# A two-layer decoder trunk on one core: the forgetting-attention half reordered, its last head overlapped with the output projection, and the last strip and norm done by token halves

## The reference, cut to what matters

```python
h = concat(meta_tokens (16), x (512))                  # 528 tokens, D_MODEL 1024
h = gla_layer(h, ...)                                  # gated linear attention, 4 heads: not touched
k, v, f_logit = split(rmsnorm(h, kv_norm_g) @ w_kv)    # 16 heads of 128
cum = cumsum(log_sigmoid(f_logit + b_forget))          # per head, over tokens
q, r = split(rmsnorm(h, norm_g) @ w_in, 2)
s = q @ k^T * 128**-0.5 + cum[q] - cum[k]              # causal
o = softmax(s) @ v                                     # per head
h = h + (o * silu(r)) @ w_out                          # 2048 -> 1024
out = rmsnorm(h, final_norm_g)[:, 16:]
```

## Time and profile before

| | |
|---|---|
| time before, median of 3 (lowest to highest) | 1192.83 us (1192.6 to 1192.99) |
| profiled execution: its own time, and its span from first to last instruction | 1195.57 us, 1193.8 us |
| PE, matmuls busy | 1107.8 us, 93% of the span |
| DVE busy, ACT busy | 612.2 us (51%), 496.3 us (42%) |
| mean granted TensorE clock | 0.965 of full |
| largest part of the chain that ended last | PE L1138, 68% |

### The profile page before, as it was taken

How to read it: one execution, slowest core, us unless ns; L and a number is a source line. 1 busy time by engine, 2 the same in 40 slices (tenths; PEclk the granted TensorE clock), 3 DMA queues, 4 the chain that set the end, 5 groups by cost and what they waited for, 6 DMA issues and landing times.

```text
span 1193.8 us, 18411 instructions
## 1 busy us (share of the span) xinstructions
PE 1107.8 (93%) x7716; PEld 1011.7 (85%) x7716; DVE 612.2 (51%) x1032; ACT 496.3 (42%) x869; POOL 0.2 (0%) x4
## 2 busy tenths in 40 slices
PE   6897999799799999999799999999999999998995
PEld 5786998799799899998688888888888888886883
DVE  5664473556457437535445554455455555564233
ACT  5624523723452325424434444444444444454221
POOL 0000000000000000000000000000000000000000
PEclk9898999899999999999899999999999999998997
DMA  6111121112112111222111222112211212211211
GB/s 224 53 54 36 54 89 54 42 65 89 37 54 80 63 54 57 103 89 71 54 66 59 71 71 71 57 68 72 71 57 68 71 55 70 72 56 51 92 50 70
DMA packets 23762, 81.77 MB, mean 68 GB/s; under 512 B 2784, under 2 KB 3040, under 8 KB 23680
## 3 DMA queue, kind: packets, MB, share of 16 engines
q1 hardware_dynamic: 23680, 80.59, 19.4%
HBM read 78.49 MB, written 2.10 MB: 68 GB/s over the span
## 4 chain that ended last, share of the span: by engine, by line
PE 83%; DVE 9%; ACT 4%; issue 3%; DMA 0%; DVEq 0%; ACTq 0%; SPq 0%
PE psum L1138 68%; PE psum L1378 3%; PE psum L1364 2%; PE psum L1207 2%; DVE w_lo L684 2%; ACT w_hi L348 1%; DVE y L691 1%; PE psum L1347 1%; PE psum L1361 1%; PE psum L1349 1%; PE psum L1350 1%; PE psum L1348 1%; DVE y L845 1%; DVE gsr L691 1%; DVE y_lo L691 1%
## 5 line engine op out<-in xcount | busy, mean ns | idle before, releaser
L684 DVE TENSOR_TENSOR w_lo<-raw,w_hi 128x1024 fp32r<-128x1024 f32 x144 | 174.9, 1220 | 81.9 <-ACT w_hi L348 81.7
L1138 PE MATMUL psum<-xh,w_hi 128*128 128x264 f32 x768 | 165.1, 297 | 35.6 <-DVE y L845 27.9
L348 ACT ACTIVATE w_hi<-raw 128x1024 fp32r<-128x1024 f32 x144 | 149.9, 1048 | 100.0 <-PE psum L1138 100.0
L1138 PE MATMUL psum<-xl,w_hi 128*128 128x264 f32 x768 | 161.0, 292 | 0.0
L1138 PE MATMUL psum<-xh,w_lo 128*128 128x264 f32 x768 | 160.0, 291 | 0.0
L1138 PEld LDWEIGHTS psum<-xh,w_hi 128*128 128x128 f32 x768 | 124.3, 197 | 40.8 <-DVE w_lo L684 29.1
L1138 PEld LDWEIGHTS psum<-xl,w_hi 128*128 128x128 f32 x768 | 124.3, 196 | 0.0
L1138 PEld LDWEIGHTS psum<-xh,w_lo 128*128 128x128 f32 x768 | 124.2, 196 | 0.0
L1138 PE MATMUL psum<-zh,w_hi 128*128 128x264 f32 x512 | 106.2, 289 | 5.9 <-DVE y L691 3.2
L1138 PE MATMUL psum<-zl,w_hi 128*128 128x264 f32 x512 | 104.4, 286 | 0.0
L1138 PE MATMUL psum<-zh,w_lo 128*128 128x264 f32 x512 | 104.1, 285 | 0.0
(11 more groups left out here) (239 smaller groups left out, 1896.8 us busy)
## 6 DMA issues: line engine op xcount, KB each, us to landing
raw<-w_all SPq DMA_DIRECT2D x144, 512.0 KB, 3.2
hT<-xT SPq DMA_DIRECT2D x8, 264.0 KB, 5.4
outT<-hT SPq DMA_DIRECT2D x8, 256.0 KB, 2.3
cst<-consts SPq DMA_DIRECT2D x1, 528.0 KB, 6.9
y<-w_up_ SPq DMA_DIRECT2D x2, 64.0 KB, 8.1
low_raw<-w_low SPq DMA_DIRECT2D x1, 64.0 KB, 2.1
f_raw<-w_f SPq DMA_DIRECT2D x1, 64.0 KB, 8.2
vec<-vecs SPq DMA_DIRECT2D x1, 22.5 KB, 1.6
```

Of the source, the lines that this page charges most:

```text
L348: nc.scalar.activation(w_hi[:, n % HI_RING, :], raw[:, n % LO_RING, :], ACT.Copy).then_inc(hi_made, 1)
L684: nc.vector.tensor_tensor(w_lo[:, n % LO_RING, :], raw[:, n % LO_RING, :], w_hi[:, n % HI_RING, :].bitcast(F32), ALU.subtract).then_inc(lo ...
L1138: i = nc.tensor.matmul(o, w[a][:, k % KT, :], x[b][:, k, c0:c1], start=k == first and a == b == 0, stop=k == last and a == 1)
```

## The change

Five things are changed.

1. **Prologue.** `q0` moves from the end of the prologue to a place right behind `LOWF`; the chunk order follows. `LOWF` gets its own place in banks 6 and 7. On ACT the last `x2h` (a part of the input of q) is made ahead of the square root; on DVE the last `x2l` and four memsets stand ahead of the reciprocal of the norm; the gate's Abs and Exp stand ahead of `keys_hi(0)`; `queries_hi(0)` and `queries_lo(0)` stand ahead of the last steps of the gate.
2. **Attends in their own bank.** `a{h}` always goes to bank 7; the other jobs alternate without it (`PLACE`, `BEFORE`). Bank 7 also holds scores, so `fox_scores(h+1)` now waits for `y` of head h (`fy_made`).
3. **Transposes.** `transpose_probs` does the ten large ones first, then the four small ones, and signals once instead of five times.
4. **Last head.** `w0`'s k-tiles 0 to 7 run between `r15` and the transposes, its k-tiles 8 to 14 between transposes and attend; then come `w1`'s 0 to 14, and then k-tile 15 of both. `z_high` and `z_low` move: 0 to 3 ahead of `q15` and 4 to 7 at the end of head 14, 8 to 14 ahead of `probs_hi(15)` and `probs_lo(15)`, and 15 alone at the end.
5. **Tail.** `w7` is computed for tokens 0 to 255 and then for 256 to 511 in a second bank (96 matmuls of 256 columns instead of 48 of 512), and add, square, sum, root, reciprocal, multiplications and stores are done per half. There are still eight stores of 256 KB; each now takes two feature tiles of half the tokens, in runs of 1 KB instead of 2 KB.

The core of the diff (the matching moves on ACT are left out, they follow the description above):

```diff
@@ -91,11 +92,23 @@
 
 
 JOBS = (["LOW"] + [j for h in range(GLA_HEADS) for j in gla_jobs(h)] + [f"W{d}" for d in range(KT)]
-        + ["k0", "LOWF", "v0", "x0", "v1", "q0"] + [j for h in range(FOX_HEADS) for j in fox_step(h)] + [f"w{d}" for d in range(KT)])
+        + ["k0", "LOWF", "q0", "v0", "x0", "v1"] + [j for h in range(FOX_HEADS) for j in fox_step(h)] + [f"w{d}" for d in range(KT)])
 JOB = {j: n for n, j in enumerate(JOBS)}
+PLACE, BEFORE = {}, {}
+_slots = 0
+for _job in JOBS:
+    if _job[0] == "a":
+        PLACE[_job] = 7
+    elif _job == "LOWF":
+        PLACE[_job] = 6
+    else:
+        PLACE[_job] = 2 * (_slots % 2)
+        _slots += 1
+    _same = [j for j in PLACE if PLACE[j] == PLACE[_job]]
+    BEFORE[_job] = _same[-2] if len(_same) > 1 else None
 
 CHUNKS = ([c for h in range(GLA_HEADS) for c in gla_strips(h)] + [f"W{d}{half}" for d in range(KT) for half in "ab"]
-          + ["k0", "v0", "v1", "q0"] + [j for h in range(FOX_HEADS) for j in fox_step(h) if j[0] in "rkqv"]
+          + ["k0", "q0", "v0", "v1"] + [j for h in range(FOX_HEADS) for j in fox_step(h) if j[0] in "rkqv"]
           + [f"w{d}{half}" for d in range(KT) for half in "ab"])
 CHUNK = {c: n for n, c in enumerate(CHUNKS)}
...
+            for half in range(2):
+                c0 = half * HS
+                for d in range(0, KT, 2):
+                    sp.wait_ge(final_made, half * KT + d + 2)
+                    sp.dma_start(out[:, d:d + 2, c0:c0 + HS], hT[:, d:d + 2, META + c0:META + c0 + HS]).then_inc(stored, 16)
             sp.wait_ge(stored, 16 * KT)
...
-                                                   op0=ALU.mult, op1=ALU.subtract).then_inc(x2l_made, 1)
-            done(dve, f"W{KT - 1}")
+                dve.wait_ge(x2h_made, d + 1)
+                nc.vector.scalar_tensor_tensor(x2l[:, d, :], hT[:, d, META:T], vec[:, G_NORM1 + d:G_NORM1 + d + 1], x2h[:, d, :].bitcast(F32),
+                                               op0=ALU.mult, op1=ALU.subtract).then_inc(x2l_made, 1)
             H = FOX_HEADS
+            nc.vector.memset(gate_all[0:64, :], 0.0).then_inc(gate_set, 1)
+            nc.vector.memset(gate_all[64:P, :], 1.0).then_inc(gate_set, 1)
+            nc.vector.memset(gate_k[64:P, :].bitcast(F32), 0.0).then_inc(gate_set, 1)
+            nc.vector.memset(gate_k[0:64, :].bitcast(F32), 1.0).then_inc(gate_set, 1)
             inverse("x2", rstd[:])
-            d = KT - 1
-            dve.wait_ge(x2h_made, d + 1)
-            nc.vector.scalar_tensor_tensor(x2l[:, d, :], hT[:, d, META:T], vec[:, G_NORM1 + d:G_NORM1 + d + 1], x2h[:, d, :].bitcast(F32),
-                                           op0=ALU.mult, op1=ALU.subtract).then_inc(x2l_made, 1)
 
             def fox_key(h):
                 done(dve, f"k{h}")
...
@@ -1049,19 +1074,22 @@
             tt(two(fb), halves(x, H), two(f_a), ALU.add, f_sum)
             dve.wait_ge(f_sum, 1)
             tt(fb, fb, rstd[0:H, :], ALU.mult, f_logit)
+            ahead("k0")
+            dve.wait_ge(f_logit, 1)
+            dve.wait_ge(f_abs, 1)
+            nc.vector.tensor_scalar(fb, fb, vec[0:H, B_F:B_F + 1], 0.0, ALU.add, ALU.min).then_inc(f_min, 1)
             keys_lo(0)
             for b in range(NBLK - 1):
                 nc.vector.memset(pr[b][:, KEYS[b]:PR_W[b]], 0.0).then_inc(pads, 1)
-            dve.wait_ge(f_logit, 1)
-            dve.wait_ge(f_abs, 1)
-            nc.vector.tensor_scalar(fb, fb, vec[0:H, B_F:B_F + 1], 0.0, ALU.add, ALU.min).then_inc(f_min, 1)
-            ahead("k0")
             dve.wait_ge(f_ln, 1)
             dve.wait_ge(f_min, 1)
             tt(f_t, fb, f_t, ALU.subtract, f_log)
             dve.wait_ge(f_log, 1)
             dve.wait_ge(gate_set, 4)
             nc.vector.tensor_tensor_scan(fb, gate_k[0:H, :].bitcast(F32), f_t, 0.0, ALU.mult, ALU.add).then_inc(f_cum, 1)
+            ahead("q0")
+            fox_query(0)
+            queries_lo(0)
             dve.wait_ge(f_chi, 1)
             dve.wait_ge(f_cum, 1)
             tt(fb, fb, gate_all[0:H, :], ALU.subtract, f_clo)
...
                     head_gate(h + 1)
                     keys_lo(h + 1)
+                else:
+                    ahead("w0a")
+                    z_low(8, H - 1)
                 probs_lo(h)
+                if h == H - 2:
+                    z_low(0, 4)
                 if h + 1 < H:
                     ahead(f"q{h + 1}")
                     fox_query(h + 1)
@@ -1101,11 +1131,14 @@
                 if h + 1 < H:
                     fox_values_lo(h + 1)
                 if h == H - 2:
-                    z_low(0, 8)
-                if h == H - 1:
-                    z_low(8, H)
-            for d in range(KT):
-                ahead(f"w{d}a")
+                    z_low(4, 8)
+            z_low(H - 1, H)
+            ahead("w0b")
+            ahead("w1a")
+            ahead("w1b")
+            for d in range(KT - 1):
+                if d >= 2:
+                    ahead(f"w{d}a")
                 done(dve, f"w{d}")
                 tt(hT[:, d, META:T], bank(slot(f"w{d}")), hT[:, d, META:T], ALU.add, o_made)
                 dve.wait_ge(osq_made, d + 1)
...
@@ -1114,12 +1147,51 @@
                 elif d > 1:
                     dve.wait_ge(oacc_made, d - 1)
                     tt(acc[:, 0:SEQ], acc[:, 0:SEQ], sq[:, d % 2, 0:SEQ], ALU.add, oacc_made)
-                ahead(f"w{d}b")
-            inverse("x3", rstd[:, 0:SEQ], SEQ)
-            dve.wait_ge(rstd_made, 7)
-            dve.wait_ge(scaled, KT)
-            for d in range(KT):
-                tt(hT[:, d, META:T], hT[:, d, META:T], rstd[:, 0:SEQ], ALU.mult, final_made)
...
+            last_add(0)
+            last_acc(0)
+            last_inverse(0)
+            last_scale(0, 0, 4)
+            last_add(1)
+            last_scale(0, 4, 6)
+            last_acc(1)
+            last_scale(0, 6, KT)
+            last_inverse(1)
+            last_scale(1, 0, KT)
...
@@ -1318,14 +1390,15 @@
             project(whole("k0"), w, xk, range(KT - 2, KT), 0, KT - 1, lambda k: pe.wait_ge(zl_made, k + 1)).then_inc(job_done, 1)
             pe.wait_ge(f_lo_made, 1)
             low_rank("LOWF", f_w[:], xk)
+            pe.wait_ge(x2l_made, KT)
+            strip_late("q0", xq)
             strip("v0", xk)
             pe.wait_ge(rstd_made, 6)
+            pe.wait_ge(f_sum, 1)
             rstd_by_token()
             pe.wait_ge(fvt_made, 1)
             transposed("x0", fvt)
             strip("v1", xk)
-            pe.wait_ge(x2l_made, KT)
-            strip_late("q0", xq)
 
             S_AT = [(7, 272), (7, 0), (6, 0), (4, 0)]
 
...
@@ -1354,16 +1428,17 @@
                 if h == 0:
                     pe.wait_ge(pads, NBLK - 1)
                 pe.wait_ge(prob_scaled, NBLK * (h + 1))
-                for j in range(NBLK + 1):
+                for j in range(NBLK):
+                    bk, c0 = PT_AT[j]
+                    c0 += 32 if j else 0
+                    for b in range(j, NBLK):
+                        nc.tensor.transpose(bank(bk, c0, c0 + BLK), pr[b][:, BLK * j:BLK * j + BLK], ident)
+                        c0 += BLK
+                for j in range(1, NBLK + 1):
                     bk, c0 = PT_AT[j]
                     rows = BLK if j < NBLK else META
-                    if j:
-                        i = nc.tensor.transpose(bank(bk, c0, c0 + 32, 0, rows), pr[j - 1][96:P, BLK * j:BLK * j + rows], ident[96:P, 96:P])
-                        c0 += 32
-                    for b in range(j, NBLK):
-                        i = nc.tensor.transpose(bank(bk, c0, c0 + BLK), pr[b][:, BLK * j:BLK * j + BLK], ident)
-                        c0 += BLK
-                    i.then_inc(prob_done, 1)
+                    i = nc.tensor.transpose(bank(bk, c0, c0 + 32, 0, rows), pr[j - 1][96:P, BLK * j:BLK * j + rows], ident[96:P, 96:P])
+                i.then_inc(prob_done, 1)
 
             def fox_attend(h):
                 job = f"a{h}"
...
@@ -1380,14 +1455,28 @@
                 i.then_inc(job_done, 1)
 
             H = FOX_HEADS
+            zs = (z_hi[:], z_lo)
+
+            def z_ready(k):
+                pe.wait_ge(zlo_made, k + 1)
+
+            def out_late(d, half, ktiles, before=None):
+                w = weights(f"w{d}{half}")
+                return project([(bank(slot(f"w{d}")), 0, SEQ)], w, zs, ktiles, 0, 15, before)
+
             for h in range(H):
                 fox_scores(h)
                 strip_late(f"r{h}", xq)
                 if h + 1 < H:
                     strip(f"k{h + 1}", xk)
+                else:
+                    wait_slot(pe, "w0")
+                    out_late(0, "a", range(0, 8), z_ready).then_inc(half_done, 1)
                 transpose_probs(h)
                 if h + 1 < H:
                     strip_late(f"q{h + 1}", xq)
+                else:
+                    out_late(0, "b", range(8, 15), z_ready)
                 fox_attend(h)
                 if h + 1 < H:
                     pe.wait_ge(fvt_made, h + 2)
...
```

(35 more changed lines are left out.)

129 lines of the change are left out of this document (81 added, 48 removed).

## The result

The changed kernel takes 1155.22 us (median of four executions, 1153.99 to 1158.04) against 1192.91 (1192.6 to 1196.08): a ratio of 0.968, 95% interval 0.9666 to 0.9694, or 37.7 us less. Four further executions beside later experiments gave 1155.32 (1154.38 to 1155.75), where seven of the kernel before had a median of 1194.48: 39.2 us less. Forecast were 1157, in a range of 1150 to 1166. The profiled execution took 1154.49 us for a span of 1152.7, 41.1 us less than the span of before.

The account below looks back on a forecast made before the run. PE was taken to bound the heads (busy 432.0 of 435 us), with waits in prologue, last head and tail. 10.3 + 10.9 + 6.7 + 3.4 + 4.3 = 35.6 us off 1192.83 gave 1157 us, range 1150 to 1166.

Parts of the forecast that it names:

- Prologue: From LOWF's end to the end of the first scores: 10.3 us saved, 12.1 if the clock holds.
- I take it that it falls again: Prologue: PE's clock drops to half after the new 2.3 us idle time before x0.
- Transposes: Each head's transposes take 1.60 us instead of 2.28: 0.68 saved per head, 10.9 us for 16 heads.
- 0.11 each: Transposes of a head: eight changes between the two sizes take 0.90 of the 2.28 us.
- The bounds with dearer small ones: Transposes: small ones at 0.17 us even in a row save 4.4 us, 1163.7, chance 18%; the skill's load rule gives 8.3.
- The one with small ones as dear as large ones: Transposes, rival: small ones go at the pace of large ones, 0.107 us; 2.6 us less saved, 1159.8; chance 8%.
- Attends in their own bank: The waits for y before strips v2 to v15 go: 14 x 0.48 = 6.7 us saved.
- Last head: Output matmuls fill idle times of 3.77 and 2.75 us; after charges, including a new wait before w2, 3.4 us saved.
- the wait before w2 is hidden: Last head, rival: PE's new wait before w2 does not show; 5.3 us less, 1151.9; chance 7%.
- Tail: From the end of the matmul stream to the span's end: 12.1 us instead of 16.3, 4.3 us saved.
- Unchanged stretch: The linear attention, 0 to 549 us, keeps its order, jobs and banks: costs nothing and gives nothing.
- the clock holds at both new idle times: Rival: no half clock after the idle times before x0 (2.3 us) and w2 (3.6); 3.5 us less, 1153.7; chance 17%.

Follow-up runs that it names:

- The experiment with the addition ahead: The changed kernel with DVE's addition of w0 moved ahead of its weight splits of w2b and w3a: 1149.57 us, ratio 0.9626 to the kernel before.

## Why the prediction was right

By its own steps:

- **Prologue, forecast 10.3, measured 12.2.** The chain was followed rightly: x0 starts 13.9 us behind LOWF's end (572.41 - 558.50), where 14.1 were forecast, and after an idle time of 2.08 where 2.3 stood. The step that was off by 1.9 us is "I take it that it falls again". It held, and the 12.1 given for that case is what came. In the three other kernels in which it did fall the piece is 25.2 us, 10.6 saved, so the forecast for that case stood too. The edit's own part is shown by the old prologue, whose piece is 35.88 again.
- **Transposes, forecast 0.68 a head, measured 0.76 to 0.77.** The mechanism was right: changes of size cost, and nearly in proportion to their number. Mis-sized was "0.11 each": a change costs 0.123 to 0.130 us, and of the 1.52 us ten large ones at 0.11 and two changes at 0.125 leave 0.17 for the four small ones, 0.04 each, where 0.07 stood. I had split the 2.28 us wrongly between the small ones and the changes. By their weight loads the small ones start 0.06 us apart (0.27 us for four, less 0.09, the length of the last), so the change into the strip behind them may cost less than the others; no run tests it alone. The bounds with dearer small ones (4.4 us, and 8.3 with small ones as dear as large ones) were wrong sums: they kept 0.11 for a change, though dearer small ones leave less of the 2.28 us for the changes. Redone they are 6.0 and about 9 us, still below the 12.3 measured, and both rivals fall. The one with small ones as dear as large ones was drawn from the Trainium skill, "TensorE: Matmul & The Clock Gate", section "LDWEIGHTS (loading the stationary operand)", by which a load of 32 rows takes as long as one of 128. The trace agrees on the length of a single load (0.13 and 0.14 us) but not on the pace: small ones start 0.06 us apart, large ones 0.11 (ten in 1.12 us). The rule that does fit is in the Trainium skill, "TensorEngine Tiling (Array Packing)", section "Key Properties": a change of the tiling mode drains TensorE. The trace agrees, with the stop of 0.17 us ahead of the first small one.
- **Attends in their own bank, forecast 6.7, measured 6.7** (18.16 less 15 x 0.767 = 11.5) in one direction and 6.5 in the other. The wait for y before the scores of head 15 is 0.23 us of idle, and with the lost overlap x to scores takes 0.94 us (1031.91 to 1032.85) where it took 0.47: 0.47 for the 0.7 charged.
- **Last head, forecast 3.4, measured 4.24 less 0.77 for its transposes = 3.5.** The wait before w2 was forecast 3.6 us, and is 3.51; the clock loss behind it 1.7, and 1.47 by the kernel that avoids it. So both sides of the sum stood, but that they met within 0.1 us is luck: the clock behind the old waits moved this piece by 1.3 us between two profiles, and the one behind the new wait by as much (see the last section). The old last head in the changed kernel costs 5.9 us in the trace and 4.4 in the medians. The experiment with the addition ahead shows that the order of three instructions on DVE, and nothing PE does, causes the new wait and its loss. The rival *the wait before w2 is hidden* priced this at 5.3 us; 5.0 was its worth in the trace (5.7 in the medians).
- **Tail, forecast 4.3, measured 5.2.** The new tail is 11.19 and not 12.1. Half 1's addition starts 0.8 us behind the stream's end at 1141.51 (1.2 forecast), and from the sum's start at 1143.81 to the root's are 0.9 us where 1.4 were set down; reciprocal and multiplications took what was said (DVE and ACT of the changed kernel):

```profile
1142.33 0.42 DVE L722 TENSOR_TENSOR hT<-psum,hT 128x256 f32<-128x256 f32 x1
...
1144.69 0.47 ACT L376 ACTIVATE sq<-psum,eps 128x256 f32<-128x256 f32 x1 [1.09 <-PE psum L1505]
...
1145.19 1.75 DVE L1176 RECIPROCAL rstd<-sq 128x256 f32<-128x256 f32 x1 [0.77 <-ACT sq L376]
...
1146.98 2.77 DVE L722 TENSOR_TENSOR hT<-hT,rstd 128x256 f32<-128x256 f32 x8
```

 Part of it is not the change's: with the old tail in the changed kernel 4.16 was lost, less 0.66 in the stream, and at one clock the halves are worth 4.3 to 4.8. The forecast terms add up to 11.95 and not to the 12.1 that stood.
- **Unchanged stretch, forecast 0.** It was 1.33 us shorter; over all the kernels LOWF's last row starts between 556.7 and 559.7. From the wait in head 3 of the linear attention on, the kernel before and the changed one take the same 116.9 us, so the difference lies ahead of it. This is the spread between executions, and it is why the sums of pieces and the differences of medians don't agree within 1 us.

The errors are 1.9 + 1.3 + 0.9 + 0.1 + 1.3 = 5.5 us in the profiled execution, all to the same side. The medians, of which the prediction spoke, moved by 37.7 us (39.2 beside the later experiments), 2.1 more than the 35.6 forecast, so 1157 came out as 1155.2: that it was so near owes something to the 3.4 us by which the two profiles lie apart from their medians. The rival that names the clock (*the clock holds at both new idle times*) was half right: it held at one and fell at the other.
